# A decoder step in float32: the gain moved from the rows to the weights, and the residual kept as transposed rows

## The chip, the cores and the metric

The kernel runs on one core of a Trainium2 chip. The metric is the device time of one execution in microseconds. A core has TensorE (PE in the rows, PEld for its weight loads), VectorE (DVE), ScalarE (ACT), GpSimd (POOL) and SyncE (SP, used here to issue DMAs). Each works through its own instructions in the order written, and they meet at semaphores. SBUF is the on-chip working memory, PSUM the small memory into which TensorE writes.

## The reference, cut to what matters

There are 1024 prompt rows and 8 sample rows of width 2048, one layer, all in float32. The two attentions between the projections are left out here, since the change does not touch what they compute.

```python
def rms_norm(x, g):
    return x * rsqrt(mean(x * x, -1) + 1e-6) * g

def layer(x, p):                                 # x: 1032 x 2048
    z = rms_norm(x, g_mix) @ w_in                # 2048 x 6656: q, k, v and gates of mixers A and B
    ya = dilated_attention(z) * silu(z_gate_a)   # three dilations, 16 heads
    yb = window_attention(z) * silu(z_gate_b)    # 16 heads on 4 kv heads, with a sink
    h = x + concat(ya, yb) @ w_out               # the residual
    gate = sigmoid(rms_norm(h, g_ple) @ w_pg)
    return rms_norm(h + (p @ w_ple) * gate, g_final)
```

## The kernel before

Activations lie transposed in SBUF: act_hi and act_lo hold 16 blocks of 128 features by 1032 rows. Each float32 is the sum of a rounded high part and a low part. Function three (L1069) forms a product from three matrix products: high weights by high rows, high weights by low rows, low weights by high rows (L1074 to L1076). A unit is one tile of 128 output columns for one third of the rows (344); it takes 16 steps of k, so 48 products. A tile is three units. Positions in the code count steps: unit u begins at position 16u, tile T at 48T.

**The head.** Nine row tiles (eight of 128 prompt rows, then the 8 sample rows) are loaded into x_in, two buffers. ScalarE squares a tile with a running sum (L1277), VectorE adds epsilon (L1587), ScalarE takes the root (L1279), and VectorE makes the inverse root and multiplies the rows by it and by the gain row g_row in one operation (L1590). TensorE transposes the result (L827), ScalarE copies it to act_hi (L1272), VectorE subtracts for act_lo (L1581). TensorE turns four tiles before its first product, and five more between products (X_LATER). The unit of the last third needs all nine.

**The in stage.** There are 52 tiles of w_in, the last two run as a pair. Weights come in groups of four blocks of k (128 by 512). SyncE loads a group into one of two places of w_raw, and waits for the group two before to be split (L427). GpSimd, group by group, rounds it to w_hi (L809) and subtracts for w_lo (L811), in a ring of five slots (WRING). TensorE waits for a group in the first unit of the tile that uses it (group_wait, L1078). For tile T the loads stand at positions 48T-12, 48T-8, 48T-4 and 48T, and bring the last group of tile T (steps 12 to 15) and the first three of tile T+1.

Function events (L167) writes the order of everything beside the products by position: copies of finished units (unit), loads (weights), the first attention (a, tiles 3 to 27), the second (b) with the samples (sa, sk), up to tile 44, and the samples of mixer B (sb, the last tiles). ScalarE, VectorE and SyncE walk one list, ALONG, sorted by position, units first; TensorE meets the same events at the same positions. Tiles 0 to 35 are copied as they are, tiles 36 on with silu.

**The out stage.** There are 16 tiles of w_out, again with a pair at the end. For the residual, SyncE loads columns of x (load_x_cols, seven DMAs for a tile), TensorE transposes them for each third of the rows (L1128), ScalarE copies them from PSUM to h_row (L1458), and VectorE adds the product (L1878), squares and sums (L1884, L1885). ScalarE issues the store of h (L1463). The gate stage, 16 tiles of w_pg with w_ple, follows.

Of the kernel before, what the change touches and what calls it, by code (L numbers as in the profile page):

```python
# [6 lines left out]
F32 = mybir.dt.float32  # L7
# [5 lines left out]
P = 128  # L13
# [33 lines left out]
X_FIRST = 4  # L47
X_LATER = {4: 4, 8: 5, 13: 6, 19: 7, 27: 8}
# [118 lines left out]
def events():  # L167
# [12 lines left out]
    for u in range(GATE0, ZPAIR):  # L180
        put(16 * u, "o_load", u)
    put(152, "a_load")
# [72 lines left out]
def build(nc, a, o):  # L255
# [12 lines left out]
    yt_dram = nc.dram_tensor("yt_scratch", [HPAIR, P, S], F32, kind="Internal").ap()  # L268
    h_dram = nc.dram_tensor("h_scratch", [KT, P, R], F32, kind="Internal").ap()
# [13 lines left out]
    with ctx:  # L283
# [10 lines left out]
        hi32 = act_hi[:].bitcast(F32)  # L294
        psum = ctx.enter_context(nc.psum_tensor("psum", [P, 8, 512], F32))

        def at(place, *tensors):
# [10 lines left out]
        x_in, x_n, g_row = at(W_END, ("x_in", [P, 2, D], F32), ("x_n", [P, 2, D], F32), ("g_row", [P, D], F32))  # L308
# [35 lines left out]
        h_stage, acc, h_row, sq, x_cols, ones, pt_hi, pt_lo, gcol = at(  # L344
            B0, ("h_stage", [P, 3, R], F32), ("acc", [P, R], F32), ("h_row", [P, 2, R], F32), ("sq", [P, T3], F32), ("x_cols", [P, 2, 9, P], F32),
            ("ones", [P, P], F32), ("pt_hi", [P, 2, R], F32R), ("pt_lo", [P, 2, R], F32R), ("gcol", [P, KT], F32))
# [71 lines left out]
        def _(sp):  # L418
# [16 lines left out]
            for i, (r0, n) in enumerate(ROW_TILES):  # L435
                if i >= 2:
                    sp.wait_ge(sem("x_normed"), i - 1)
                sp.dma_start(x_in[0:n, i % 2, :], x_p[r0:r0 + n, :] if i < 8 else x_s).then_inc(sem(f"x_loaded{i % 2}"), 16)
                if i == 0:
                    sp.dma_start(ident[:], a["c_ident"]).then_inc(sem("consts"), 16)  # L440
                    sp.wait_ge(sem("x_loaded0"), 16)
                    sp.dma_start(g_row[:], bcast_rows(a["g_mix"][0:1, :], P)).then_inc(sem("consts"), 16)
                elif i == 1:
                    sp.dma_start(pick[:], a["c_pick"]).then_inc(sem("consts"), 16)
                elif i == 6:
                    sp.wait_ge(sem("consts"), 48)
                    sp.dma_start(gcol[:], a["g_ple"].rearrange("a (k p) -> p (a k)", p=P), allow_slow_non_contiguous=True).then_inc(sem("consts"), 16)
                for g in {1: (0, 1), 2: (2,), 3: (3,), 5: (4,)}.get(i, ()):
                    weights(g)
            for g in range(5, 7):  # L450
                weights(g)

# [228 lines left out]
            def load_x_cols(i):  # L681
                par = i % 2
                if i >= 2:
                    sp.wait_ge(sem("r_turned"), 3 * (i - 1))
                cols = slice(i * P, i * P + P)
                for t in range(2):
                    q0 = T3 * t
                    sp.dma_start(x_cols[:, par, 3 * t:3 * t + 2, :], x_p[q0:q0 + 256, cols].rearrange("(c p) n -> p c n", p=P)).then_inc(sem(f"xc_loaded{par}"), 16)
                    sp.dma_start(x_cols[0:88, par, 3 * t + 2, :], x_p[q0 + 256:q0 + 344, cols]).then_inc(sem(f"xc_loaded{par}"), 16)
                sp.dma_start(x_cols[:, par, 6:8, :], x_p[688:944, cols].rearrange("(c p) n -> p c n", p=P)).then_inc(sem(f"xc_loaded{par}"), 16)  # L690
# [37 lines left out]
            for k in range(HPAIR):  # L728
                if k >= 3:
                    sp.wait_ge(sem("h_split"), k - 2)  # L730
# [83 lines left out]
        def _(pe):  # L814
# [269 lines left out]
            for u in range(ZPAIR):  # L1084
                tile, t = divmod(u, 3)
                if u < 3:
                    pe.wait_ge(sem("x_lo"), 4 * (3, 6, len(ROW_TILES))[u])
# [893 lines left out]
```

## Time and profile before

| what | value |
|---|---|
| median of 3 runs | 2392.67 us (2391.92 to 2398.38) |
| profiled execution | 2398.78 us, of which the span of the trace is 2397.0 us |
| mean granted TensorE clock | 0.992 |
| PE busy | 2341.2 us, 98% of the span |
| ACT busy | 637.2 us, 27% |
| DVE busy | 830.6 us, 35% |
| POOL busy | 768.4 us, 32% |
| DMA packets moved | 294.25 MB |

The profile is one execution, in us from the span's start. Its page lists each engine's busy time, the chain of work that ended last, followed back from the end, and groups of instructions by line. A wait is put down to what released it. Other views show instructions in order of time, groups by shape, and busy time in a stretch with the clock granted to TensorE (1.00 is 2.4 GHz, 0.50 is 1.2 GHz).

### The profile page before, as it was taken

The numbers are of one execution on the slowest core, as the hardware profiler recorded it, in microseconds if no ns is written. First come the engines' busy times: TensorE is split into PE (matmuls) and PEld (weight loads), VectorE is DVE, ScalarE is ACT, GpSimd is POOL, SyncE is SP. The second block draws the span as 40 slices with busy tenths as digits, with TensorE's granted clock in tenths as the row PEclk, the third lists the DMA queues.
The fourth block names the chain that finished last, engine by engine and source line by source line (L and its number), as shares of the span: only waits on it lengthen the run. The fifth ranks groups of instructions, "written<-read, shape, count | busy, mean of one in ns | idle before, by whom it ended". The sixth has DMA issues, their size and how long they took to land.

```text
span 2397.0 us, 40204 instructions
## 1 busy us (share of the span) xinstructions
PE 2341.2 (98%) x16009; PEld 2229.2 (93%) x16009; DVE 830.6 (35%) x2232; ACT 637.2 (27%) x1881; POOL 768.4 (32%) x783
## 2 busy tenths in 40 slices
PE   5999999999999999999999999999999999999997
PEld 4999999999999999888888999999999999999996
DVE  7013333233333404444555434242212262211253
ACT  5122222222222312223444310210000132222444
POOL 2332222222222132221222223333333334454564
PEclk8999999999999999999999999999999999999998
DMA  5233233333333325444454454533323344333685
GB/s 191 65 113 98 78 104 96 80 110 96 82 106 90 88 78 151 134 134 142 144 164 143 129 172 126 178 114 94 98 86 96 122 146 129 106 112 103 176 246 190
DMA packets 383795, 294.25 MB, mean 123 GB/s; under 512 B 53807, under 2 KB 347927, under 8 KB 382319
## 3 DMA queue, kind: packets, MB, share of 16 engines
q1 hardware_dynamic: 342261, 249.43, 35.6%
q10 hardware_dynamic: 41347, 42.25, 5.3%
q8 instruction: 127, 2.08, 0.4%
q14 instruction: 60, 0.49, 0.1%
HBM read 225.38 MB, written 66.22 MB: 122 GB/s over the span
## 4 chain that ended last, share of the span: by engine, by line
PE 90%; DVE 4%; DMA 3%; ACT 1%; POOL 1%; SPq 0%; issue 0%; DVEq 0%; ACTq 0%; POOLq 0%
PE psum L1074 26%; PE psum L1076 25%; PE psum L1075 25%; PE psum L855 3%; PE psum L877 2%; PE psum L888 2%; PE psum L962 1%; PE psum L949 1%; PE psum L932 1%; DMA y_in<-yt_scratch 1%; DVE x_n L1590 1%; PE psum L914 1%; DVE act_lo L1581 1%; PE psum L1214 1%; PE psum L1128 1%; PE psum L979 1%
## 5 line engine op out<-in xcount | busy, mean ns | idle before, releaser
L1074 PE MATMUL psum<-act_hi,w_hi 128*128 128x344 f32 x4032 | 1313.3, 326 | 2.6 <-DVE act_lo L1859 0.9
L1076 PE MATMUL psum<-act_hi,w_lo 128*128 128x344 f32 x4032 | 1288.4, 320 | 0.0
L1075 PE MATMUL psum<-act_lo,w_hi 128*128 128x344 f32 x4032 | 1287.2, 319 | 0.0
L1074 PEld LDWEIGHTS psum<-act_hi,w_hi 128*128 128x128 f32 x4032 | 759.5, 188 | 13.4 <-issue 9.8
L1075 PEld LDWEIGHTS psum<-act_lo,w_hi 128*128 128x128 f32 x4032 | 758.9, 188 | 0.2
L1076 PEld LDWEIGHTS psum<-act_hi,w_lo 128*128 128x128 f32 x4032 | 758.6, 188 | 0.0
L809 POOL CAST w_hi<-w_raw 128x512 fp32r<-128x512 f32 (+1 forms) x352 | 225.1, 639 | 1519.7 <-PE psum L1076 1356.8
L811 POOL TENSOR_TENSOR w_lo<-w_raw,w_hi 128x512 fp32r<-128x512 f32 (+1 forms) x390 | 504.5, 1294 | 63.5 <-ACT w_hi L1529 35.1
L1673 DVE COPY prob_t<-psum 128x512 f32<-128x512 f32 (+1 forms) x56 | 35.5, 635 | 448.8 <-PE psum L888 448.8
L1943 DVE TENSOR_TENSOR t_gate<-psum,acc 128x344 f32<-128x344 f32 x48 | 24.8, 516 | 255.9 <-PE psum L1076 255.9
L1878 DVE TENSOR_TENSOR h_row<-psum,h_row 128x344 f32<-128x344 f32 x48 | 22.9, 516 | 243.9 <-PE psum L1076 230.8
L1335 ACT ACTIVATE prob_t<-psum 128x512 f32<-128x512 f32 (+1 forms) x56 | 30.9, 551 | 233.8 <-PE psum L888 233.8
L1324 ACT ACTIVATE prob<-prob,near 128x256 f32<-128x256 f32 (+3 forms) x128 | 72.1, 564 | 77.2 <-DVE near L1658 77.2
L1296 ACT ACTIVATE stage<-psum 128x344 f32<-128x344 f32 (+1 forms) x108 | 48.4, 448 | 155.7 <-PE psum L1076 154.6
L1708 DVE CUSTOM_DVE_ANT_0 prob_b<-psum,bias_b 128x256 f32<-128x256 f32 (+1 forms) x128 | 44.5, 404 | 122.7 <-PE psum L962 65.6
L1458 ACT ACTIVATE h_row<-psum 128x344 f32<-128x344 f32 x48 | 21.9, 457 | 234.4 <-PE psum L1128 200.5
L1538 ACT ACTIVATE t_gate<-t_gate 128x344 f32<-128x344 f32 x48 | 23.5, 490 | 210.3 <-DVE t_gate L1943 208.5
L1367 ACT ACTIVATE probt_b<-psum 128x512 f32<-128x512 f32 (+1 forms) x64 | 36.5, 571 | 159.1 <-PE psum L962 159.0
L1802 DVE TENSOR_TENSOR stage<-stage,o_in 128x344 f32<-128x344 f32 (+1 forms) x42 | 27.4, 653 | 132.6 <-ACT stage L1303 116.2
L855 PE MATMUL psum<-zk,zq 64*128 64x128 f32 (+3 forms) x416 | 67.3, 443 | 0.0
L1645 DVE CUSTOM_DVE_ANT_0 prob<-psum,bias 128x256 f32<-128x256 f32 (+3 forms) x128 | 58.2, 501 | 19.4 <-PE psum L855 19.4
L1376 ACT ACTIVATE prob_b<-prob_b,mx 128x256 f32<-128x256 f32 (+1 forms) x128 | 61.4, 481 | 0.0
(212 smaller groups left out, 1982.9 us busy)
## 6 DMA issues: line engine op xcount, KB each, us to landing
w_raw<-in_w_in SPq DMA_DIRECT2D x208, 256.0 KB, 3.0
w_raw<-in_w_pg SPq DMA_DIRECT2D x94, 256.0 KB, 3.0
w_raw<-in_w_out SPq DMA_DIRECT2D x64, 256.0 KB, 2.7
z_scratch<-stage ACTq DMA_DIRECT2D x72, 172.0 KB, 1.9
h_scratch<-h_row ACTq DMA_DIRECT2D x16, 516.0 KB, 2.7
x_in<-in_x_prompt SPq DMA_DIRECT2D x8, 1024.0 KB, 5.0
zq<-z_scratch SPq DMA_DIRECT2D x32, 256.0 KB, 4.3
o_scratch<-ot SPq DMA_DIRECT2D x32, 256.0 KB, 3.4
```

Source lines behind the costliest of these rows:

```text
L809: pool.tensor_copy(w_hi[:, slot, 0:n], raw(g, n)).then_inc(sem("w_rounded"), 1)
L811: pool.tensor_tensor(w_lo[:, slot, 0:n], raw(g, n), w_hi[:, slot, 0:n].bitcast(F32), ALU.subtract).then_inc(sem("w_split"), 1)
L855: mm = pe.matmul(psum[:, 2 + h, col:col + w], queries(half), keys(half), start=True, stop=True)
L877: mm = pe.matmul(psum[HD * h:HD * h + HD, 6, c0:c1:step], values[:, HD * h:HD * h + HD], prob_t[:, h, x * P:(x + 1) * P], start=(c in (1, ...
L888: mm = pe.transpose(psum[:, 4 + h, x * P:(x + 1) * P], prob_of(n, c)[:, h, x * P:(x + 1) * P], ident[:])
L1074: pe.matmul(psum[:, bank, 0:T3], hi_w, hi_a[:, k, rows], start=(k == 0), stop=False, skip_group_check=True)
L1075: pe.matmul(psum[:, bank, 0:T3], hi_w, lo_a[:, k, rows], start=False, stop=False, skip_group_check=True)
L1076: return pe.matmul(psum[:, bank, 0:T3], lo_w, hi_a[:, k, rows], start=False, stop=stop, skip_group_check=True)
L1296: act.activation(stage[:, slot, 0:w], psum[:, u % 2, 0:w], ACT.Copy).then_inc(sem("bank_free"), 1)
L1324: m = act.activation(piece, piece, ACT.Exp, bias=st[:, 2 + h:3 + h], accum_out=st[:, 4 + h:5 + h])
L1376: mm = act.activation(pr, pr, ACT.Exp, bias=m[:, 4 + h:5 + h], accum_out=m[:, 6 + h:7 + h])
L1645: m = dve.tensor_tensor_reduce(pr[:, h, col:col + nk], psum[:, 2 + h, col:col + nk], bias[:, h, u0:u0 + nk], SCALE, -3e38, ALU.add, ALU.ma ...
```

## The change

The product of the norm with w_in is (x * r) * g @ w = (x * r) @ (g * w), r being the inverse root of a row and g the gain of a feature.

1. In the head VectorE multiplies the rows by r alone (tensor_scalar). x_in has three buffers, the sample rows come first (HEAD), ScalarE takes the root straight from its own sum, and ident and the gains (16 columns g_mix) are loaded from ScalarE's queue. The gain row and the waits for constants are gone. TensorE turns five tiles, the samples' among them, before its first product.
2. GpSimd multiplies the first five weight groups by the gains, ScalarE all others of w_in: four activations of 128 by 128 a group. GpSimd's rounding waits for them. In ALONG the gains of a tile T stand at positions 48T+2, +6, +10 and +14, 14 steps behind their loads.
3. The transposed rows x * r, high and low, are stored to memory during tiles 3 to 19 (x_save, two DMAs of 516 KB for a block of features), and so are the roots. In the out stage SyncE loads both parts (load_residual) and the roots once, and VectorE adds the parts and multiplies by the root. The loads of x columns, the transposes and ScalarE's copies are gone.

Some semaphores are shared under new names (rows_loaded, meaned, rooted, y_hi); left out of the diff.

```diff
-X_FIRST = 4
-X_LATER = {4: 4, 8: 5, 13: 6, 19: 7, 27: 8}
+HEAD = [8, 0, 1, 2, 3, 4, 5, 6, 7]
+X_FIRST = 5
+X_LATER = {6: 5, 13: 6, 15: 7, 22: 8}
+X_NEEDED = (4, 7, 9)
+GAINED_FIRST = 5
...
+    for k in range(KT):
+        put(16 * (11 + 3 * k) + 5, "x_save", k)
+    for g in range(7, WG * (NZ - 2) + 7):
+        tile, part = divmod(g - 7, WG)
+        put(16 * (3 * tile + 2) + 4 * (part + 1) + 14, "gain", g)
...
+            for j, i in enumerate(HEAD):
+                r0, n = ROW_TILES[i]
+                if j >= 3:
+                    sp.wait_ge(sem("x_normed"), j - 2)
+                sp.dma_start(x_in[0:n, j % 3, :], x_p[r0:r0 + n, :] if i < 8 else x_s).then_inc(sem(f"rows_loaded{j % 3}"), 16)
+                for g in {1: (0,), 2: (1,), 4: (2,), 5: (3,), 7: (4,)}.get(j, ()):
                     weights(g)
...
+                elif e[0] == "x_save":
+                    k = e[1]
+                    sp.wait_ge(sem("x_lo"), 4 * len(HEAD))
+                    sp.dma_start(xh_dram[k], hi32[:, k, :]).then_inc(sem("x_saved"), 16)
+                    sp.dma_start(xl_dram[k], lo32[:, k, :]).then_inc(sem("x_saved"), 16)
...
-            def load_x_cols(i):
+            def load_residual(i):
                 par = i % 2
                 if i >= 2:
+                    sp.wait_ge(sem(f"h_stored{par}"), 16 * (i // 2))
+                    sp.wait_ge(sem("h_summed"), 3 * (i - 1))
+                sp.dma_start(h_row[:, par], xh_dram[i]).then_inc(sem(f"xh_loaded{par}"), 16)
+                if i:
+                    sp.wait_ge(sem("r_ready"), i)
+                sp.dma_start(x_low[:], xl_dram[i]).then_inc(sem("xl_loaded"), 16)
...
+            def gain(g):                         # GpSimd, groups 0 to 4
+                pool.wait_ge(sem(f"w_loaded{place}"), 16 * count)
+                gains = g_mix[:, k:k + n].rearrange("p (x a) -> p x a", a=1).to_broadcast([P, n, P])
+                pool.tensor_tensor(raw(g, n), raw(g, n), gains, ALU.mult).then_inc(sem("w_gained_first"), 1)
...
+                    if g < GAINED_FIRST:
+                        pool.wait_ge(sem("w_gained_first"), g + 1)
+                    elif what == "in":
+                        pool.wait_ge(sem("w_gained"), g - GAINED_FIRST + 1)
                     pool.tensor_copy(w_hi[:, slot, 0:n], raw(g, n)).then_inc(sem("w_rounded"), 1)
...
-                for x, (c0, n) in enumerate(PIECES[t]):
-                    mm = pe.transpose(psum[:, 4, c0:c0 + n], x_cols[0:n, i % 2, 3 * t + x, :], ident[0:n, 0:n])
-                mm.then_inc(sem("r_turned"), 1)
...
+                act.activation(x_sq[0:n], x_in[0:n, j % 3, :], ACT.Square, accum_out=small[0:n, i:i + 1]).then_inc(sem("x_squared"), 1)
+                act.wait_ge(sem("x_squared"), j + 1)
+                act.activation(small[0:n, 9 + i:10 + i], small[0:n, i:i + 1], ACT.Sqrt, bias=small[0:n, 61:62], scale=1.0 / D).then_inc(sem("rooted"), 1)
...
+            def gain(g):                         # ScalarE, groups 5 to 207
+                act.wait_ge(sem(f"w_loaded{place}"), 16 * count)
+                for x in range(n):
+                    m = act.activation(raw(g, n)[:, x, :], raw(g, n)[:, x, :], ACT.Copy, scale=g_mix[:, k + x:k + x + 1])
+                m.then_inc(sem("w_gained"), 1)
...
                 if e[0] == "unit":
                     unit(e[1])
+                elif e[0] == "gain":
+                    gain(e[1])
...
-                act.activation(h_row[:, i % 2, T3 * t:T3 * (t + 1)], psum[:, 4, 0:T3], ACT.Copy).then_inc(sem("r_copied"), 1)
...
-                dve.scalar_tensor_tensor(x_n[0:n, i % 2, :], x_in[0:n, i % 2, :], small[0:n, 18 + i:19 + i], g_row[0:n, :],
-                                         ALU.mult, ALU.mult).then_inc(sem("x_normed"), 1)
+                dve.tensor_scalar(x_n[0:n, j % 2, :], x_in[0:n, j % 3, :], small[0:n, 18 + i:19 + i], None, ALU.mult).then_inc(sem("x_normed"), 1)
...
+            def residual(i):
+                par = i % 2
+                dve.wait_ge(sem(f"xh_loaded{par}"), 16 * (i // 2 + 1))
+                dve.wait_ge(sem("xl_loaded"), 16 * (i + 1))
+                chain(dve.tensor_tensor(h_row[:, par, :], h_row[:, par, :], x_low[:], ALU.add))
+                dve.tensor_tensor(h_row[:, par, :], h_row[:, par, :], x_rms[:], ALU.mult).then_inc(sem("r_ready"), 1)
```

## Rows read from the trace of the kernel before

**Rows 1.** The page, part 1: busy us, share of the span, instructions.

```profile
PE 2341.2 (98%) x16009; PEld 2229.2 (93%) x16009; DVE 830.6 (35%) x2232; ACT 637.2 (27%) x1881; POOL 768.4 (32%) x783
```

**Rows 2.** The head in order of time (start us, us, engine, line, operation, tiles).

```profile
13.31 0.15 DVE L1587 TENSOR_SCALAR small<-small 128x1 f32<-128x1 f32 x1 [12.45 <-DMA pick<-in_c_pick]
...
31.12 2.35 DVE L1590 SCALAR_TENSOR_TENSOR x_n<-x_in,small,g_row 128x2048 f32<-128x2048 f32 x1
33.39 2.48 DVE L1581 TENSOR_TENSOR act_lo<-psum,act_hi 128x512 fp32r<-128x512 f32 x4
...
36.85 0.64 PE L1074 MATMUL psum<-act_hi,w_hi 128*128 128x344 f32 x1
...
37.04 2.35 DVE L1590 SCALAR_TENSOR_TENSOR x_n<-x_in,small,g_row 128x2048 f32<-128x2048 f32 x1
...
39.83 1.91 PE L827 MATMUL psum<-ident,x_n 128*128 128x128 f32 x16
```

**Rows 3.** TensorE at the start of the third unit.

```profile
67.03 0.32 PE L1074 MATMUL psum<-act_hi,w_hi 128*128 128x344 f32 x1
```

**Rows 4.** Groups by line and shape (busy us, mean ns of one, idle before).

```profile
L1784 DVE TENSOR_SCALAR bprob<-bprob 16x1032 f32<-16x1032 f32 x1 | 0.7, 687 | 0.0
...
L1277 ACT ACTIVATE x_n<-x_in 128x2048 f32<-128x2048 f32 x8 | 15.3, 1916 | 5.4 <-DMA x_in<-in_x_prompt 5.4
...
L1503 ACT ACTIVATE f_lo<-psum 128x128 f32<-128x128 f32 x26 | 5.7, 275 | 0.0
```

**Rows 5.** TensorE in the out stage, around two of the 48 turns.

```profile
1629.47 0.46 PE L1128 MATMUL psum<-ident,x_cols 128*128 128x128 f32 x3
...
1629.96 0.32 PE L1075 MATMUL psum<-act_lo,w_hi 128*128 128x344 f32 x1
...
1914.84 0.52 PE L1128 MATMUL psum<-ident,x_cols 128*128 128x128 f32 x3 [1.39 <-ACT h_row L1458]
```

**Rows 6.** TensorE at tile 20: its first product and that of step 12.

```profile
624.94 0.32 PE L1074 MATMUL psum<-act_hi,w_hi 128*128 128x344 f32 x1
...
630.60 0.32 PE L1074 MATMUL psum<-act_hi,w_hi 128*128 128x344 f32 x1
```

**Rows 7.** ScalarE at tile 20.

```profile
629.18 0.48 ACT L1321 ACTIVATE near<-n_stat,near 128x1 f32<-128x1 f32 x2 [5.73 <-DVE near L1658]
...
631.77 0.33 ACTq L1298 DMA_DIRECT2D z_scratch<-stage  x1
```

**Rows 8.** GpSimd ahead of tile 20: its last group rounded and subtracted.

```profile
622.29 0.61 POOL L809 CAST w_hi<-w_raw 128x512 fp32r<-128x512 f32 x1 [1.91 <-DMA w_raw<-in_w_in]
622.98 1.28 POOL L811 TENSOR_TENSOR w_lo<-w_raw,w_hi 128x512 fp32r<-128x512 f32 x1
```

**Rows 9.** VectorE at tile 20: one operation twice.

```profile
624.72 0.16 DVE L1620 TENSOR_TENSOR n_w<-near 128x2 f32<-128x2 f32 x1
...
626.32 0.95 DVE L1620 TENSOR_TENSOR n_w<-near 128x2 f32<-128x2 f32 x1
```

**Rows 10.** Busy time by stretch (us; PE, PEld, DVE, ACT, POOL, granted clock, DMA, GB/s).

```profile
2319.40:2322.10 2.70, 0.28 (x2) 0.03 (x1) 0.00 (x0) 1.40 (x9) 0.72 (x1) 1.00 0.66 184
2322.60:2326.00 3.40, 3.24 (x13) 2.77 (x12) 0.74 (x2) 2.44 (x5) 2.86 (x3) 0.50 0.78 263
...
1914.80:1918.20 3.40, 3.36 (x22) 3.37 (x23) 1.78 (x3) 2.19 (x2) 1.20 (x1) 1.00 0.91 288
```

**Rows 11.** ScalarE's unit copy at tile 40, and TensorE's step 12 there.

```profile
1249.40 0.45 ACT L1303 ACTIVATE stage<-psum 128x336 f32<-128x336 f32 x1
...
1250.50 0.32 PE L1074 MATMUL psum<-act_hi,w_hi 128*128 128x344 f32 x1
```

**Rows 12.** ScalarE at tile 49, just behind its unit copy.

```profile
1489.04 1.28 ACT L1432 ACT_TABLE_LOAD   x1
1491.28 1.06 ACT L1432 ACTIVATE bprob<-bprob 16x1032 f32<-16x1032 f32 x1 [0.95 <-DVE bprob L1789]
```

**Rows 13.** DMA issues by size (median us to landing).

```profile
w_raw<-in_w_in SPq DMA_DIRECT2D x208, 256.0 KB, 3.0
```

More of the change, by code:

```diff
@@ L797, in _, with split @@
         def _(pool):
-            for g, (what, i, k, n) in enumerate(GROUPS):
+            def gain(g):
+                what, i, k, n = GROUPS[g]
+                place, count, _ = RAW[g]
+                if g == 0:
+                    pool.wait_ge(sem("gain_loaded"), 16)
+                pool.wait_ge(sem(f"w_loaded{place}"), 16 * count)
+                gains = g_mix[:, k:k + n].rearrange("p (x a) -> p x a", a=1).to_broadcast([P, n, P])
+                pool.tensor_tensor(raw(g, n), raw(g, n), gains, ALU.mult).then_inc(sem("w_gained_first"), 1)
+            def split(g):
+                what, i, k, n = GROUPS[g]
                 place, count, _ = RAW[g]
@@ L811, in _ @@
                 pool.tensor_tensor(w_lo[:, slot, 0:n], raw(g, n), w_hi[:, slot, 0:n].bitcast(F32), ALU.subtract).then_inc(sem("w_split"), 1)
+            for g in range(len(GROUPS)):
+                if g < GAINED_FIRST:
+                    gain(g)
+                split(g)
         @block.tensor
         def _(pe):
-            pe.wait_ge(sem("consts"), 48)
+            pe.wait_ge(sem("ident_loaded"), 16)
             def x_turn(i):
-                r0, n = ROW_TILES[i]
+                r0, n = ROW_TILES[HEAD[i]]
                 pe.wait_ge(sem("x_normed"), i + 1)
@@ L1151, in _ @@
                         continue
-                    if k % WG == WG - 1 and k < KT - 1:
-                        residual(i, k // WG)
                     if i == 0:
@@ L1178, in _ @@
                     group_wait("out", HPAIR + i, k)
-                    if i == 0 and k % 2 and 3 <= k < 15:
-                        residual(HPAIR + (k - 3) // 6, (k - 3) // 2 % 3)
                     for t in range(3):
@@ L1284, in _ @@
             act.wait_ge(sem("x_lo"), 36)
+            act.wait_ge(sem("gain_loaded"), 16)
+            def gain(g):
+                what, i, k, n = GROUPS[g]
+                place, count, _ = RAW[g]
+                act.wait_ge(sem(f"w_loaded{place}"), 16 * count)
+                for x in range(n):
+                    m = act.activation(raw(g, n)[:, x, :], raw(g, n)[:, x, :], ACT.Copy, scale=g_mix[:, k + x:k + x + 1])
+                m.then_inc(sem("w_gained"), 1)
+            for g in range(GAINED_FIRST, 7):
+                gain(g)
             def unit(u):
@@ L1433, in _ @@
                     act.activation(brow[:, 2, :], brow[:, 2, :], ACT.Exp).then_inc(sem("s_exped"), 1)
+            act.wait_ge(sem("x_saved"), 32 * KT)
             for k in range(HPAIR):
-                act.wait_ge(sem(f"y_loaded{k % 3}"), 16 * (k // 3 + 1))
+                if k == 2 * WG:
+                    gain(GROUP["out", 0, 0] - 1)
+                act.wait_ge(sem(f"rows_loaded{k % 3}"), 16 * (k // 3 + 1 + len(HEAD) // 3))
                 act.wait_ge(sem("x_used"), k + 1)
@@ L1465, in _ @@
             for i in range(HPAIR):
-                for t in range(3):
-                    residual(i, t)
                 h_store(i)
@@ L1567, in chain, with inverse_root @@
                 dve.wait_ge(sem("dve_chain"), done[0])
-            def inverse_root(n, square, root, out):
+            def inverse_root(square, root, out):
                 chain(dve.reciprocal(out, root))
```

157 lines of the change are left out of this document (71 added, 86 removed).

## The prediction

> **What bounds the kernel now.** The page first: TensorE is busy for 2341 of 2397 us [rows 1]. The view of busy time by stretch and the order of TensorE's instructions then show that from the third unit (67.0 us) to the second attention it never stops: a step of k, three products, takes 0.47 us (12 steps in 5.66 us) [rows 6]. So the time is work on TensorE plus the few places where it waits: the head, and single waits of 1 to 3 us. An edit pays only if it takes instructions from TensorE or shortens the head, and costs only if TensorE comes to wait. I therefore read next, for each helper, how long before TensorE's need it is done.
>
> **The head.** VectorE sets its pace. From one multiplication of a tile's rows to the next lie 5.92 us: 2.35 for it, 2.48 for four low parts, 1.1 for small operations [rows 2]. Before the first of them it waits until 13.3 us for a constant's DMA. After the change that wait is gone. The new multiplication has one tensor and no gain row; no row has its shape, the nearest is a multiplication by a constant, 1032 elements in 0.69 us [rows 4], which gives 1.2 us for 2048; the other end is the old 2.35 us. I take 1.2, so a cycle is 4.7 us. ScalarE's share, 1.9 for the square [rows 4] plus root and four copies, is just under this. I lay the tiles out: samples normed at 7.6 us, the next four at 11.0, 14.5, 19.6 and 24.0, and the fifth turned at 27.8, where the first product starts (36.85 before) [rows 2]. The last four are normed at 28.6, 33.0, 38.8 and 43.8, each before TensorE asks. From first product to third unit are then 32 steps of 0.47, four turns of 1.9 [rows 2] and about 1.2 us at the lower clock: third unit at 51.8, against 67.03 [rows 3]. That is 15.2 us. Five gains of about 1.3 us on GpSimd now run beside, and VectorE operations get longer beside GpSimd (0.16 becomes 0.95 us [rows 9]), so I take **-13.5**, between -9 (old multiplication time) and -16.
>
> The Trainium skill, SBUF — State Buffer, section "SBUF: two separate sides", says that VectorE in a 2-port mode or with two SBUF inputs, and a GpSimd operation, hold one port pair exclusively, so that the later one waits for the whole of the other. By that rule the new multiplication would still queue behind a GpSimd operation of 1.3 us; if four in the head do, the head gives 5 us less and the sum is 2409. The long operation of rows 9 beside GpSimd's work agrees with it; how often they meet in the new head no row shows.
>
> **The out stage.** Each third of a tile's residual costs TensorE three transposes: from their start to the second product behind them lie 0.49 us, in which one product of 0.157 stands [rows 5]. That is 0.33 us, 48 times: 15.9 us, all on TensorE's path. One of them also waited for ScalarE, which stood behind a load: 1.39 us idle, 1.6 with the restart [rows 5]. **-17.5**. Instead VectorE gets two operations of 1032 elements a tile, about 2.5 us by the low parts' rate [rows 2], and SyncE two DMAs. Loads for tile i+1 are issued when tile i ends, behind GpSimd's last split, and are needed a tile (22.6 us) later; the first residual comes late (some 8 us into tile 1), yet its banks are wanted only at tile 2. I cost these at nothing; if that cover fails, TensorE waits once for about 5 us. The x_save stores stand behind the one load that is urgent and before loads with 20 us to spare; nothing too.
>
> **The gains, which stand in a chain that had slack.** The last group of tile T is needed at step 12, 5.66 us into the tile at the least [rows 6]. Before, GpSimd finished it ahead of the tile (at tile 20: 624.3 against a need at 630.6) [rows 6, 8]. Now ScalarE must first reach the gain at position 48T+2, which stands behind the copy of the unit that just ended and all of its attention work ordered before. A gain is four activations of 128 by 128, at 0.275 each [rows 4], overlapping by 0.05 to 0.09: I take 0.9 (0.8 to 1.1). Then come GpSimd's 1.97 from rounding to split [rows 8]. In a plain tile ScalarE, 0.3 us behind TensorE, takes 0.45 for the copy and 0.33 for the store [rows 7, 11] and is done at about 1.1 us, the group at 4.0: no wait, 1.7 us of slack. But at tile 20 ScalarE stands in the exponentials of an attention step until VectorE releases it at 629.18, and is through with copy and store only at 632.1 [rows 7]. Add 0.9 and 2.0: 635.0, 4.4 us after the need. GpSimd's own work at that moment falls away, since it waits too; VectorE's lengthened operations there shrink by 0.8 [rows 9], and two before them by 0.6. I take a wait of **3.0** (between 1.5 and 4.6). Position puts tiles 8, 11, 14, 17, 20 and 23 in the same place of the attention's cycle, and ScalarE is as late there in each. Six times 3.0 is 18.
>
> After a wait of 2.7 us the trace shows the granted clock at 0.50 for 3.4 us, and 13 products in them against 22 in an equal stretch at 1.00; after the wait of 1.6 us before 1914.8 the clock stayed at 1.00 [rows 10]. I charge 1.55 us for each of the six: 9.3.
>
> Other tiles: at tile 40 ScalarE ends the copy at 1249.85, so the group comes at 1252.7 against 1250.50 [rows 11]: 2.2. Tile 42 is alike (exponentials ordered at its start): 2.2, and one lower clock between the two: 1.5. Three more (5, 30, 44), read in the same way, together 2.0 (0 to 4). At tile 49 the third gain stands before the exponential of mixer B's samples, and must wait for its load, which SyncE issues only when the late group is split: from 1489.0, gain 0.9, split 2.0, landing 3.0 [rows 13], gain 0.9, table load 1.28 [rows 12] gives 1497.1 for the exponential that ran at 1491.28, and TensorE already waits for it: 5.9. In the second attention ScalarE also stands in this way, up to 3 us, before steps whose results TensorE wants some 5 us later: 0.8 (0 to 20). Gains in sum: 18 + 9.3 + 5.9 + 2.0 + 5.9 + 0.8 = **+42**.
>
> **The sum.** -13.5 - 17.5 + 42 = +11. On the profiled execution, 2398.8, that is 2409.8; on the median of the runs, 6.1 lower, **2404**. Removed work is certain, added waiting is estimated: about 32 us are given and 42 taken.
>
> **The rivals.**
> *The waits are covered (faster).* If ScalarE comes to the gain no later than 1.7 us after a plain tile's copy, the group is in time. At the six tiles it comes 5 us too late for that today, but this lateness is a wait for VectorE, itself slowed by GpSimd. Should it vanish, 27.3 us go: +11 - 27 = -16, or 2377. It decides at 3 us: if VectorE releases ScalarE before 626.2 instead of 629.2, tile 20 shows no wait. Against it: I find 1.4 us of slowing, not 3.
> *The clock stays.* Waits as forecast, but like the one of 1.6 us they leave the clock at 1.00: 10 us less, 2394, no difference.
> *A crowded second attention.* ScalarE's gains and waits for loads spoil each of 14 tiles by 1.5 us: +20, 2424. For it: ScalarE blocks in order. Against: transposed probabilities have nearly 5 us.
> *The multiplication is no faster than with the gain row.* The change then doesn't do what it says in the head: 1.15 us on eight tiles, less what overlaps, 5 to 8 us: 2411.
>
> **How the numbers follow.** Chances: forecast 0.43, waits covered 0.17, clock stays 0.17, crowded 0.13, slow multiplication 0.10. The forecast's own range, from a wait of 2 us to one of 4 at the six tiles and -16 to -10 in the head, is 2393 to 2416. The range for 8 in 10 leaves out most of the first and part of the third: 2381 to 2424. A measurement of this kernel tells about 0.3%, 7 us. Slower by more: most of forecast, crowded and slow multiplication, 0.58. Faster by more: the covered case and a little of the clock's, 0.20. Between: 0.22.
>
> **What would show it.** The third unit near 52 us; no line of transposes in the out stage and 157 ns between products there; at tiles 8 to 23, each third, a wait of TensorE on GpSimd's w_lo at step 12 of some 3 us with a clock of 0.50 behind it; one wait of over 7 us in tile 49; ScalarE's gain 0.9 us a group. I am wrong if w_lo is never waited for in the in stage (then VectorE freed ScalarE early), or if the head still ends after 58 us, or if waits on ScalarE's copies appear throughout tiles 30 to 43.

## The result, and the profile of the changed kernel

Four runs of the changed kernel have a median of 2465.16 us (2461.73 to 2472.34), four of the kernel before 2393.97 (2391.92 to 2398.38). The ratio is **1.030, 95% interval 1.0286 to 1.031: 71 us slower**. The profiled execution took 2461.73 us with a span of 2459.8. The forecast was 2404 in a range up to 2424: the sign was right, the size was not. The traces below lie 8 us closer together than the medians, since the profiled execution of the kernel before was 4.8 us above its median and that of the changed kernel 3.4 below.

First the page, its busy times (engine, busy us, share, instructions) and two of its costliest groups (line, engine, operation, tiles, count, then busy us and mean ns of one, then idle time before it and its cause):

```profile
PE 2349.1 (95%) x15865; PEld 2231.9 (91%) x15865; DVE 842.0 (34%) x2265; ACT 859.6 (35%) x2645; POOL 771.4 (31%) x788
...
L1113 PE MATMUL psum<-act_hi,w_hi 128*128 128x344 f32 x4032 | 1319.3, 327 | 35.7 <-POOL w_lo L843 26.3
...
L1315 ACT ACTIVATE w_raw<-w_raw,small 128x128 f32<-128x128 f32 x812 | 254.7, 390 | 247.2 <-DMA w_raw<-in_w_in 231.9
```

TensorE has 144 instructions fewer than before [rows 1] (the turns are gone) and is still busy 8 us longer: its clock was low more often (mean granted clock 0.981). The last row is the new work: 812 multiplications of 128 by 128 on ScalarE, 390 ns each.

The view of TensorE's waits, over the whole span (engine, line, what it waited for: us in total, times, longest):

```profile
PE psum L1113 <- POOL w_lo L843: 27.6, 14, 3.7
PE psum L864 <- DVE x_n L1621: 16.0, 6, 7.9
PE psum L1009 <- DMA zv<-z_scratch: 13.6, 2, 10.3
PE psum L1084 <- DVE bprob L1825: 8.0, 1, 8.0
PE psum L1029 <- DVE s_prob L1777: 5.4, 3, 2.9
PE psum L1113 <- DVE act_lo L1890: 4.5, 1, 4.5
PE psum L1113 <- DVE h_row L1917: 3.8, 2, 3.2
PE psum L986 <- ACT probt_b L1402: 3.7, 3, 2.2
```

The second row is the head. The first is the six waits that were forecast (20.6 us) and eight small ones. The third, over 10 us at one place, on a **DMA**, was in no case of the prediction.

Where each microsecond went can be read without any theory: both kernels execute the same 4128 groups of three products in the same order, so I take the start of the first product of each tile in both traces and subtract. Negative is ahead of the kernel before; the changes between rows are what a stretch gained or lost.

```
first product of              before   changed   difference   change since the row above
tile 0                         36.86     28.78      -8.1
tile 1                         74.57     60.38     -14.2      head                    -14.2
tile 8                        260.62    246.97     -13.7      tile 5                   +0.5
tile 24                       745.35    763.88     +18.5      tiles 8,11,14,17,20,23  +32.2
tile 28                       871.79    892.08     +20.3      tiles 25 to 27           +1.8
tile 45                      1394.15   1459.04     +64.9      second attention        +44.6
last pair (tile 50)          1519.41   1591.22     +71.8      tile 49                  +6.9
out stage, tile 1            1589.52   1666.16     +76.6      out tile 0               +4.8
out stage, last pair         1898.68   1962.39     +63.7      13 tiles at -0.99       -12.9
gate stage                   1947.73   2007.78     +60.1      the pair                 -3.7
last product                 2378.01   2441.26     +63.2      gate stage               +3.2
```

The last line, +63.2, is the difference of the two profiled spans (62.8) but for 0.4 us. The head and the removed transposes give time, as forecast; the losses lie between, and about half of them in one stage, the second attention (tiles 28 to 45), where 0.8 us plus 5.9 at tiles 40 and 42 were forecast.

**What happens in the second attention.** The largest single loss is in tile 37. TensorE (the view of the instructions that use the tile zv: durations, first and last start, then who waited):

```profile
L1009 PE MATMUL psum<-ident,zv x4: 421/421/473, 1191.6 to 1192.3; 128*128 128x128 f32 x4
L493 SPq DMA_DIRECT2D zv<-z_scratch x2: 455/526/597, 1187.4 to 1187.9; - x2
...
  PE psum L1009: 10.3, 1
```

The data were asked for 4 us before they were used, at 1187.4, and TensorE had nothing to do from 1181.3. SyncE issues this load. Its queue in order of time, first in the changed kernel, then in the kernel before at the same place (start us, us from the start of the first issue to the end of the last, queue, line, transfer, count):

```profile
1170.50 0.33 SPq L668 DMA_DIRECT2D yt_scratch<-stage  x1
1171.65 15.12 SPq L442 DMA_DIRECT2D w_raw<-in_w_in  x3
1186.87 0.45 SPq L662 DMA_DIRECT2D o_in<-o_scratch  x1
1187.36 1.09 SPq L493 DMA_DIRECT2D zv<-z_scratch  x2
```

```profile
1137.05 0.50 SPq L653 DMA_DIRECT2D yt_scratch<-stage  x1
1140.43 5.17 SPq L429 DMA_DIRECT2D w_raw<-in_w_in  x3
1145.71 0.46 SPq L647 DMA_DIRECT2D o_in<-o_scratch  x1
1146.21 1.09 SPq L483 DMA_DIRECT2D zv<-z_scratch  x2
```

Three weight loads take SyncE 15.12 us instead of 5.17, because a load of a group waits until the group two before it, which lay in the same place of w_raw, has been split by GpSimd. The load of zv behind them is issued 12.0 us into the tile (which starts at 1175.37) instead of 1.7 (1144.52 before): 10.3 us later, as much as TensorE waits. And the split waits for ScalarE (changed kernel, ScalarE, then GpSimd):

```profile
1180.63 0.57 ACT L1434 ACTIVATE v_nat<-psum 128x512 f32<-128x512 f32 x1
1181.11 2.43 ACT L1315 ACTIVATE w_raw<-w_raw,small 128x128 f32<-128x128 f32 x8
```

```profile
1169.95 1.67 POOL L843 TENSOR_TENSOR w_lo<-w_raw,w_hi 128x512 fp32r<-128x512 f32 x1
1182.53 0.61 POOL L841 CAST w_hi<-w_raw 128x512 fp32r<-128x512 f32 x1 [10.91 <-ACT w_raw L1315]
```

GpSimd stands for 10.91 us until ScalarE, through with an attention step, comes to the multiplications at 1181.11. So the chain is: ScalarE's order, GpSimd's split, SyncE's queue, and behind the weight loads in that queue the attention's own loads, which have nothing to do with the weights. TensorE waits at the end of it. I call this **theory S**.

### The profile page after: what moved, and what is told of

Same layout as the page of the kernel before. It is cut to its first block, busy times and chain, and to the rows that moved or that the text cites. A ratio compares the mean times of both kernels' runs of the same rounds, so it can differ in the third digit from the quotient of the medians.

```text
span 2459.8 us, 40657 instructions
## 1 busy us (share of the span) xinstructions
PE 2349.1 (95%) x15865; PEld 2231.9 (91%) x15865; DVE 842.0 (34%) x2265; ACT 859.6 (35%) x2645; POOL 771.4 (31%) x788
## 4 chain that ended last, share of the span: by engine, by line
PE 76%; DVE 7%; DMA 6%; ACT 6%; POOL 3%; issue 2%; SPq 1%; ACTq 0%; DVEq 0%; POOLq 0%
PE psum L1113 22%; PE psum L1115 21%; PE psum L1114 21%; PE psum L892 3%; PE psum L925 2%; PE psum L914 2%; POOL w_lo L843 2%; ACT w_raw L1315 1%; DMA w_raw<-in_w_ple 1%; ACT prob_b L1411 1%; DMA w_raw<-in_w_in 1%; POOL w_hi L841 1%; DMA w_raw_more<-in_w_ple 1%; DVE prob_b L1739 1%; PE psum L999 1%
## 5 line engine op out<-in xcount | busy, mean ns | idle before, releaser
L1315 ACT ACTIVATE w_raw<-w_raw,small 128x128 f32<-128x128 f32 x812 | 254.7, 390 | 247.2 <-DMA w_raw<-in_w_in 231.9
L1833 DVE TENSOR_TENSOR stage<-stage,o_in 128x344 f32<-128x344 f32 (+1 forms) x42 | 21.6, 514 | 161.9 <-ACT stage L1338 155.3
L1917 DVE TENSOR_TENSOR h_row<-psum,h_row 128x344 f32<-128x344 f32 x48 | 22.0, 511 | 130.1 <-PE psum L1115 130.1
```

What stands on the lines that cost most here:

```text
L1315: m = act.activation(raw(g, n)[:, x, :], raw(g, n)[:, x, :], ACT.Copy, scale=g_mix[:, k + x:k + x + 1])
```

## The experiments

Each kernel was run once, beside the kernel before on the same chip (2393.3 to 2394.9 us), except the last, which was run five times. Four runs of the changed kernel lie up to 10.6 us apart, so a single time tells little; the differences by tile tell more. The kernel with all three moves was profiled twice: its two traces agree to 0.1 us from tile 1 to tile 49, and then differ by 1.4 us in tile 49 and by 3.0 each at the first out tile and in the gate stage. Three rivals to S: **A**, ScalarE, standing in order in front of a multiplication until its weights land, holds up the attention's exponentials; **W**, ScalarE simply has 255 us more to do; **D**, the saved rows crowd the attention's transfers. A difference below is that of tile starts to the kernel before, as in the table above. The "first" of a tile's four multiplications is the one at position 48T+2, for the last group of tile T itself; the second, third and fourth are for the first groups of tile T+1.

### Without the multiplications

```diff
-                    if g < GAINED_FIRST:
-                        pool.wait_ge(sem("w_gained_first"), g + 1)
-                    elif what == "in":
-                        pool.wait_ge(sem("w_gained"), g - GAINED_FIRST + 1)
...
-                elif e[0] == "gain":
-                    gain(e[1])
```

(and the other calls of gain.)

> The changed kernel without any multiplication by g_mix (that part of the computation is left out; everything else of the change stays, the saved rows too). Theory G (everything that the in stage lost comes from where the multiplications stand): the head stays 14.2 us ahead of the kernel before, and the 33 us of the six tiles 8, 11, 14, 17, 20 and 23, the 46 us of the second attention and the 7 us of tile 49 all go; what is left is the out stage's own difference, so the time is near 2376 us. Rival D (the rows saved to memory crowd the attention's transfers): the second attention keeps much of its 46 us, time 2390 to 2422, TensorE's waits on z_scratch and s_ring stay at 10 us and more.

2366.0 us. The difference is -15.8 at tile 1 and stays at -15.8 up to the start of tile 49: the whole loss of the in stage up to there, second attention included, is the multiplications'. Of the 6.9 us of tile 49 2.3 stay, against the expectation. The saved rows are still stored here, so **D falls**. The expected 2376 was 10 us too high: I had taken the losses at the first out tile and in the gate stage (+4.8, +3.2) for separate ones, and they went too.

### The later groups' multiplications later; then their loads too

Two kernels. In the first, the third and fourth group's multiplication stand 12 steps later, so that ScalarE no longer waits in front of them in the second attention:

```diff
-        put(16 * (3 * tile + 2) + 4 * (part + 1) + 14, "gain", g)
+        put(16 * (3 * tile + 2) + 4 * (part + 1) + (14, 14, 26, 26)[part], "gain", g)
```

The second has this and a later place in SyncE's order for the loads of the same two groups:

```diff
-        put(16 * (3 * tile + 2) + 4 * (part + 1), "weights", g)
+        put(16 * (3 * tile + 2) + 4 * (part + 1) + (0, 0, 16, 16)[part], "weights", g)
```

> The multiplications of the third and fourth group of each tile stand 12 steps later in ScalarE's order, so ScalarE no longer waits in front of them for the weights; loads and everything on SyncE stay. The six waits of tiles 8 to 23 stay in every case (33 us), they hang on the first group. Theory S (SyncE's queue stands behind the weight loads that wait for the late split, and with it the attention's loads): the second attention keeps over 35 of its 46 us, TensorE's wait of 10 us on z_scratch at tile 37 stays, time 2452 to 2468. Theory A (ScalarE, waiting in order for the weights, holds the attention's exponentials): the second attention loses under 15 us, time 2420 to 2435.

> As the kernel with the third and fourth multiplication 12 steps later, and SyncE also issues these two groups' loads 16 steps later, when the splits that they wait for are done, so that SyncE's queue no longer stands. Theory S: the wait of 10 us at tile 37 goes and the second attention's loss falls from 46 to under 15 us, time 2420 to 2435; the six waits (33 us) stay. Theory A: the same as the kernel with the later multiplications alone, to 5 us. Rival D (saved rows crowd the transfers) or W (ScalarE simply has 255 us more to do): over 30 of the 46 us stay in both kernels.

2457.3 and 2420.5 us. Between tiles 28 and 45 the first lost 44.6 us (22.75 to 67.38), as much as the changed kernel; the second lost 4.9 (23.23 to 28.17). The waits of TensorE in the second attention (940 to 1420 us), first kernel, its largest:

```profile
PE psum L1009 <- DMA zv<-z_scratch: 16.8, 3, 10.8
```

and all that the second one has:

```profile
PE psum L1113 <- POOL w_lo L843: 3.4, 3, 1.9
PE psum L1029 <- DVE s_prob L1777: 0.5, 1, 0.5
```

ScalarE's order is the same in both; only SyncE's differs. **S holds, A falls** (its time for the first kernel was 2420 to 2435). ScalarE's waits for weights say the same: from 940 to 1420 us they were 17 with 45.1 us in the changed kernel, and the first kernel has none and loses as much. SyncE's own waits around tile 37 (1140 to 1200 us), changed kernel, first and second, in this order:

```profile
SPq L442 <- POOL w_lo L843: 29.2, 6, 12.5
```

```profile
SPq L442 <- POOL w_lo L843: 36.5, 6, 12.6
```

```profile
SPq L442 <- POOL w_lo L843: 16.3, 7, 5.3
```

### The first group's multiplication earlier

```diff
-        put(16 * (3 * tile + 2) + 4 * (part + 1) + 14, "gain", g)
+        put(16 * (3 * tile + 2) + 4 * (part + 1) + (8, 14, 14, 14)[part], "gain", g)
```

> The multiplication of the first group of each tile stands 6 steps earlier in ScalarE's order, ahead of the first attention's last step of a head instead of behind it. All theories: the six waits of 3.6 us on w_lo at tiles 8, 11, 14, 17, 20 and 23 go with their clock losses, -33 us, and the 7 us of tile 49 may go too. Theory S: the third group's load waits for the first group's split, so SyncE is released earlier too and the second attention loses 15 to 30 us instead of 46: time 2400 to 2418. Theory A: ScalarE still waits in front of the later groups and the second attention keeps over 38 us: time 2424 to 2434.

2416.3 us, in S's range. The six waits are gone entirely: the difference is -14.85 from tile 1 to tile 30. But the second attention still lost 39.2 us, where S had 15 to 30 and A over 38. Taken alone this part spoke for A. The trace shows why S's number was wrong and not S: SyncE now goes sooner past the load that waits for the first group's split, and stands at the next one, which waits for the **second** group's split, whose multiplication I had not moved:

```profile
1130.84 0.33 SPq L668 DMA_DIRECT2D yt_scratch<-stage  x1
1131.99 13.49 SPq L442 DMA_DIRECT2D w_raw<-in_w_in  x3
1145.57 0.45 SPq L662 DMA_DIRECT2D o_in<-o_scratch  x1
```

13.49 us instead of 15.12. A queue that stands at several places in a row is not freed by clearing one of them.

### The same waits with almost no work in them

```diff
-                for x in range(n):
-                    m = act.activation(raw(g, n)[:, x, :], raw(g, n)[:, x, :], ACT.Copy, scale=g_mix[:, k + x:k + x + 1])
+                m = act.activation(raw(g, n)[:, 0, 0:1], raw(g, n)[:, 0, 0:1], ACT.Copy, scale=g_mix[:, k:k + 1])
```

> Each of ScalarE's multiplications is shrunk to one instruction on one column of one block (so g_mix is left out of the groups from the sixth on); its waits, its place in ScalarE's order and GpSimd's wait for it stay. Theory S (the place does it, through the late split and SyncE's queue): with 1 to 2 us less per group the six waits shrink from 3.6 to about 2.5 us each and the second attention keeps 20 to 46 us; time 2425 to 2455. Rival W (ScalarE's 255 us of extra work do it): both fall to nothing, time 2366 to 2380.

2435.6 us. The longest wait on w_lo fell from 3.7 to 2.4 us, the six places together from +32.2 to +23.7, the second attention from +44.6 to +34.1. So of the 99 us between the changed kernel and the one without multiplications, some 30 hang on their duration and 70 on their place, with one instruction of 291 ns left in each. **W falls** as the main cause.

### The first out tile

At the start of the out stage SyncE loads the attentions' output (y_in, L718), and ScalarE rounds it to act_hi in 14 "row copies". In their midst stands the multiplication of the last w_in group.

```diff
-                if k == 2 * WG:
+                if k == 2 * WG - 2:
                     gain(GROUP["out", 0, 0] - 1)
```

> The changed kernel with one edit: the multiplication of the last w_in group stands two row copies earlier (before the seventh row copy and not before the ninth) in ScalarE's order at the start of the out stage. Theory Q (the 4.7 us at the first out tile are SyncE's queue: the row loads stand behind a weight load that waits for this group's split): the wait for act_lo falls from 4.5 us to under 1.5 and the time to 2459 to 2462. Rival R (the rows, or the first saved residual, are late for another reason): the wait stays at 4 to 5 us and the time at 2465.

2460.7 us; the wait on act_lo L1890 is 1.9 us instead of 4.5, and the step at out tile 0 is +1.6 instead of +4.8. The wait missed "under 1.5" by 0.4, and neither the total nor a step that two traces of one kernel show 3.0 apart would prove it. The other kernels settle it: in the five with this multiplication at its old place (the changed one, the two with later groups, the early first group, the shrunk multiplications) the wait is 3.1 to 5.3 us, in the six traces with it two copies earlier (this one and all that follow with the three moves) it is 0 to 2.0. **Q holds.** R's saved residual is not it: TensorE waits for no h_row at this place. What the 1.9 us left hang on no run shows (0.87 in the kernel before).

### All multiplications on GpSimd

```diff
-                if g < GAINED_FIRST:
+                if GROUPS[g][0] == "in":
                     gain(g)
```

(with ScalarE's calls left out.)

> GpSimd multiplies all w_in groups by g_mix itself, just ahead of its cast, as it does for the first five; ScalarE multiplies none. Theory S: the split no longer waits for ScalarE's order, so nothing is late as long as GpSimd keeps up (1.3 us more per group on an engine that is busy about a third of the time): near the kernel without multiplications, 2366 to 2376 us. Rival: the split that comes 1.3 us later holds the weight loads and through SyncE the attention's loads after all, 2385 to 2400 us.

2394.1 us, the rival's range, but for half of it not by its mechanism. The kernel is 28.0 us behind the one without multiplications at the last product; 14.0 of that it loses at tiles 8 to 23. There SyncE was not held longer: from 230 to 760 us it waited 364.5 us for splits, against 358.4. Of TensorE's waits in the first attention (240 to 800 us) there is one kind, six times:

```profile
PE psum L1111 <- ACT stage L1327: 9.2, 6, 1.7
```

ScalarE's copy comes late because VectorE's softmax steps ahead of it take longer beside GpSimd. VectorE and GpSimd at tile 8:

```profile
245.86 0.16 DVE L1643 TENSOR_TENSOR n_w<-near 128x2 f32<-128x2 f32 x1
245.94 1.46 DVE L1646 TENSOR_SCALAR prob<-prob,near 128x256 f32<-128x256 f32 x2
...
248.27 1.14 DVE L1643 TENSOR_TENSOR n_w<-near 128x2 f32<-128x2 f32 x1
```

```profile
246.21 1.04 POOL L823 TENSOR_TENSOR w_raw<-w_raw,small 128x512 f32<-128x512 f32 x1 [0.79 <-DMA w_raw<-in_w_in]
...
248.11 1.29 POOL L841 TENSOR_TENSOR w_lo<-w_raw,w_hi 128x512 fp32r<-128x512 f32 x1
```

The scaling of two pieces takes 1.46 us beside the multiplication that starts at 246.21; in the kernel without multiplications the same scaling takes 0.61. The small operation at 248.27 takes 1.14 instead of 0.16 and ends with GpSimd's subtraction for the low part, at 249.4; such a meeting the kernel without multiplications has too. VectorE's results are ready at 252.2 instead of 249.0, in a tile that starts 0.6 us later. VectorE was busy 922.9 us in all against 865.5 there. This is the pair of ports that the prediction named for the head: the Trainium skill, SBUF — State Buffer, "SBUF: two separate sides", says the later of the two engines waits for the whole instruction of the other, and the trace agrees, with 1.14 us for an operation of 0.16.

In the second attention the kernel loses 7.2 us more. There SyncE's waits for splits are longer (from 880 to 1400 us 241.2 us against 211.2), and one of TensorE's waits, 1.6 us, is for zv, so the rival's own mechanism may have a part; no run separates the two.

### The three moves together

First group 6 steps earlier, third and fourth 12 later with loads 16 later, last group two copies earlier.

> The three moves together: first group's multiplication 6 steps earlier, third and fourth 12 steps later with their loads 16 steps later on SyncE, and the last w_in group's multiplication two row copies earlier. If the moves act on separate losses they add up: head -14.2, six waits gone, second attention +8, tile 49 +1.4, first out tile +0, out stage -15: 2376 to 2384 us. If the early first group again holds ScalarE in the second attention (the kernel with it alone had +33 there), 2395 to 2405 us.

2369.7 us, 6 below the expected range and 24 below the kernel before. The difference is -13.9 from tile 1 to 26, -10.95 at tile 45, -23.1 at the last pair of the out stage, -28.7 at the end. The second attention loses nothing, where +8 was expected. The page and the waits over the whole span:

```profile
PE 2321.9 (98%) x15865; PEld 2211.3 (93%) x15865; DVE 858.7 (36%) x2265; ACT 857.4 (36%) x2645; POOL 773.5 (33%) x788
```

```profile
PE psum L864 <- DVE x_n L1621: 16.0, 6, 8.3
PE psum L925 <- DVE prob L1640: 2.6, 1, 2.6
PE psum L1236 <- DVE t_y L1994: 2.2, 1, 2.2
PE psum L1218 <- DVE acc L1924: 2.1, 1, 2.1
PE psum L1084 <- DVE bprob L1825: 2.1, 1, 2.1
```

ScalarE does the same 857 us of work as in the changed kernel (859.6). Only the order of some multiplications and loads is another, and 92 us of the span are gone: this rules out W. ScalarE even waits longer for weights than in the changed kernel (54.6 us from 940 to 1420 us, against 45.1) at no cost to TensorE, which A could not explain. The second wait (with the clock behind it 4.0 us) is not in the kernel without multiplications: it is for VectorE, which waits for the load of the tile f_w in the first attention. SyncE issued it 3.1 us later against the tile than there, and it took 5.8 us to land instead of 4.2.

### The head, piece by piece

Three kernels put back one part of the old head each, on top of the three moves (third unit there at 53.07 us, in the changed kernel 52.74, before 67.03 [rows 3]).

The constant pick loaded behind the second row tile again, and TensorE waiting for it:

> The three-move kernel, with the constant pick loaded right behind the second row tile again and TensorE's first instruction waiting for it, as before the change. Theory H1 (most of the head's gain is the shorter cycle on VectorE): the third unit comes at most 2 us later than in the three-move kernel. Rival H2 (most of it is this wait): 5 to 9 us later, total 2375 to 2379.

2371.2 us; the third unit at 53.26. With pick alone loaded early and waited for, 0.2 us are lost.

A multiplication with a second tensor:

```diff
-                dve.tensor_scalar(x_n[0:n, j % 2, :], x_in[0:n, j % 3, :], small[0:n, 18 + i:19 + i], None, ALU.mult)
+                dve.scalar_tensor_tensor(x_n[0:n, j % 2, :], x_in[0:n, j % 3, :], small[0:n, 18 + i:19 + i], x_in[0:n, j % 3, :], ALU.mult, ALU.mult)
```

> The three-move kernel, with the rows' scaling in the form with a second tensor (the rows themselves, so they are also multiplied by themselves, which the reference does not do), as long as the old multiplication by the gain row. Theory H1: each scaling takes 2.35 us again and the third unit comes 5 to 8 us later, total 2375 to 2378. If the scaling was not on the path, 0 to 2 us.

2379.7 us; the third unit at 60.61, 7.5 us later.

The gain row's broadcast and VectorE's wait:

> The three-move kernel, with the old gain row's broadcast load (1 MB) behind the first row tile again (written to a spare stretch of memory and not used) and the constant pick behind the second, and VectorE waiting for both before its first row statistic, as before the change; the short multiplication stays. Theory H3 (what the multiplication does not explain of the head's gain, 6.3 us, is this wait and load): the third unit comes 4 to 7 us later than in the three-move kernel, total 2374 to 2377. Rival H4 (it is the third row buffer, the rows' order and the fewer small operations): 0 to 2 us later.

2378.9 us; the third unit at 61.43, 8.4 us later, above the expected 4 to 7. VectorE's first statistic stands until 13.95, as it did until 13.31 before [rows 2]. Since pick alone cost 0.2 us, it is the 1 MB of the gain row ahead of it that makes the wait. The two parts, 7.5 and 8.4, add to more than the whole (14.0), so they are not independent of each other, or something else of the new head costs about 2 us; the row order and the third row buffer were not tried alone.

### The three moves, timed

> The three-move kernel again, timed in rounds against the kernel before: 2370 us, ratio 0.990 (0.987 to 0.992), if the first look holds.

The kernel is that of the three moves, unchanged. Five runs have a median of 2373.05 us (2369.91 to 2377.86), nine of the kernel before 2394.89 (2392.76 to 2397.01): ratio 0.9913, interval 0.9899 to 0.9926. **It beats both kernels**: 22 us below the kernel before and 92 below the changed one.

## Why the prediction was right and where it was wrong

**The head: right.** -13.5 forecast, -14.2 measured; third unit 51.8 forecast, 52.74 measured (its first product, and VectorE's eight multiplications as a group):

```profile
52.74 0.40 PE L1113 MATMUL psum<-act_hi,w_hi 128*128 128x344 f32 x1 [0.41 <-ACT stage L1331]
...
L1621 DVE TENSOR_SCALAR x_n<-x_in,small 128x2048 f32<-128x2048 f32 x8 | 12.1, 1516 | 0.3
```

The multiplication took 1.27 to 2.02 us (1.2 taken, from a 1032-element row), 1.5 in the mean, and both named causes, the shorter operation and the wait that is gone, proved real when put back singly. Three of the eight took 1.64 to 2.02 us and the others 1.29 to 1.32; if that is the queueing behind GpSimd for which the prediction had 5 us, it came to 1.8.

**The out stage: right in its removed work.** -0.99 us a tile, 3 times 0.33 as forecast, 13 times; -3.7 in the pair, where 2.0 for six turns and 1.6 for the stall were the terms. With out tile 0's own 0.99 that makes the 17.5. Not covered, though costed at nothing, was the start of the stage: 5.8 us gross at out tile 0. The prediction named that price ("once for about 5 us") and gave it to the residual; what came late was the attentions' output y_in, through SyncE's queue. The +3.2 of the gate stage is a wait of 3.2 us for h_row L1917. It can't be given to the change: of the two traces of the three-move kernel one has no such wait and the other one of 2.3 us. What decides it stays open.

**The six tiles: right in place and mechanism, short in size.** 27.3 forecast, 32.2 measured: five times 5.2 and once 6.2 (tile 17). ScalarE at tile 20 (which starts at 633.12 here), to be read beside [rows 7]:

```profile
635.92 0.48 ACT L1356 ACTIVATE near<-n_stat,near 128x1 f32<-128x1 f32 x2 [4.29 <-DVE near L1689]
...
638.51 0.33 ACTq L1333 DMA_DIRECT2D z_scratch<-stage  x1
638.88 2.44 ACT L1315 ACTIVATE w_raw<-w_raw,small 128x128 f32<-128x128 f32 x8 [0.40 <-ACT stage L1331]
```

VectorE frees ScalarE 2.80 us into the tile, 1.4 earlier than before (4.24), as the prediction had from the lengthened operations. What was mis-sized is the multiplication: 1.28 us for a group of four (2.44 for the eight of two groups) where 0.9 was taken from a copy of 275 ns out of PSUM. The wait became 3.4 to 3.7 us instead of 3.0 (from start to start of the products 3.55 or more, for they overlap by 0.16). The clock then was as forecast: 0.60 granted in the 3.6 us behind the wait, 14 products in them, and 0.98 with 31 instructions in the 3.4 after:

```profile
642.30:645.90 3.60, 3.58 (x14) 0.60 0.32 93
646.30:649.70 3.40, 3.40 (x31) 0.98 0.36 105
```

So +5.2 us are 3.55 for the wait and 1.6 for the clock (1.55 forecast). At tile 17 the wait was no longer, but the granted clock stood at 0.50 for 6.8 us instead of 3.4, which cost 2.7. The first multiplication of the tile moved ahead of the attention step takes all of it away, at six places at once.

**Tile 49: right in mechanism, with some luck in the number.** +6.9 measured, 5.9 forecast; the chain of split, load, multiplication and table load is there as it was laid out, with 1.28 instead of 0.9 for the multiplication. But 2.3 of the 6.9 stay when the multiplications are left out, and what those are no run shows.

**The second attention: wrong, and it is most of the miss.** +44.6 against 0.8 and the 5.9 at tiles 40 and 42: some 38 of the 52 us between the forecast +11 and the +63.2 of the traces. The rest is the first out tile (5.8), the six tiles (4.9), the gate stage (3.2) and tile 49 (1.0), less 0.7 in the head. The step that failed is the sentence "In the second attention ScalarE also stands in this way, up to 3 us, before steps whose results TensorE wants some 5 us later: 0.8 (0 to 20)". It asked only what ScalarE's lateness does to ScalarE's own results, and put the rest at nothing without following it. It did not follow the late split on to who waits for it: SyncE, which issues the next weight load only then, and behind it, in one queue, the loads of the attention. The prediction had just this step for tile 49 ("which SyncE issues only when the late group is split") and for the rival priced at +20, named the wrong engine ("ScalarE blocks in order"). The runs put 40 of the 44.6 us on SyncE's order (the two kernels with later multiplications, which differ in that alone). Of this stage's loss 33.0 us are TensorE's waits (15, of 0.5 to 10.3 us, 34.6 in sum, against 1.6 in the kernel before), and 11.6 are longer products: by my estimate some 10 of them from the clock, which stood at 0.50 five times behind a wait, for 3.4 us or more; from 940 to 1400 us the granted clock was 0.97 against 1.00 before.

**The rivals.** The waits were not covered, the clock did not stay, and the multiplication with one tensor was faster; these three fell as the forecast said. The fourth, the crowded second attention, had the right place, a wrong engine and half the price: its upper bound, +20 us, rested on ScalarE's own lateness of 3 us, while SyncE's queue could stand for 15.

## What to carry to other kernels

When a step is put into a producer's chain, follow its result to everyone who waits for it, and for each of these ask what else stands behind the waiting instruction in its in-order queue. Here the engine that issues transfers waited for a buffer to come free, and the loads behind it served another stage; three moves in hand-written orders turned a kernel 3% slower into one 0.9% faster with the same work. A shorter operation would not have done it: with almost no work left in the multiplications their place still cost 70 us. A way to read it quickly: compare the starts of the same instruction in both traces tile by tile, then look at the issuing queue's waits in the stretch where the difference grows.

## What the runs showed of the hardware that was not expected

- ScalarE's copy of 128 by 128 with a factor per partition, from SBUF to SBUF, is 390 ns in the profile and follows its neighbour in 0.30 (1.28 for four, 2.43 for eight); the copy of the same size out of PSUM was 275 ns [rows 4].
- GpSimd's multiplication of 128 by 512 took 1.04 us against 1.28 for ScalarE's four; by itself it is the shorter, but a scaling on VectorE that met it took 1.46 us instead of 0.61.
- The clock's price differed between equal waits. Five waits of 3.4 to 3.7 us in the changed kernel cost 1.4 to 1.7 us more by the clock, and one of 3.4 (tile 17) cost 2.7. In the kernel with GpSimd's multiplications waits of 1.6 us (tiles 11, 14, 20 and 23) cost 1.9 us with the clock staying at 1.00 at tiles 11 and 20, and 3.5 with 3.4 us at 0.50 behind them at tiles 14 and 23. Nothing in these rows tells the two kinds apart.
